# Root and reciprocal taken on one number per token and head, in the key and the group normalisation

## The reference, cut to what matters

```python
hs = lambda u: u.reshape(b, t, RWKV_HEADS, RWKV_HEAD)
kk = hs(k * k_k)
kk = kk * lax.rsqrt(jnp.maximum(jnp.sum(kk * kk, -1, keepdims=True), 1e-24))   # key normalisation
...
mu_y = y.mean(-1, keepdims=True)                                               # y: output of the scan
var_y = jnp.square(y - mu_y).mean(-1, keepdims=True)
y = ((y - mu_y) * lax.rsqrt(var_y + GN_EPS)).reshape(b, t, RWKV_DIM) * lnx_g + lnx_b   # group normalisation
```

## Time and profile before

| | us |
|---|---|
| median of 3 runs | 4569.9 |
| the three runs | 4568.84, 4569.9, 4578.2 |
| the profiled execution, its own time | 4578.92 |
| its span | 4577.1 |
| `project_pairs` early, late | about 145 to 305, 1160 to 1555 |
| `scan_pairs` early, late | about 305 to 560, 1555 to 2190 |
| busy: PE, DVE, ACT, POOL | 3770.9, 3228.8, 883.7, 1830.5 |

### The profile page before, as it was taken

The page is one execution under the profiler, slowest core; times in us unless marked ns, Lnnn a source line. Parts: engine busy times, 40 slices in busy tenths (PEclk is TensorE's granted clock), DMA queues, the critical chain, the costliest instruction groups (busy, mean ns, idle before and its releaser), DMA issues. The chain is left out here.

```text
span 4577.1 us, 70268 instructions
## 1 busy us (share of the span) xinstructions
PE 3770.9 (82%) x27402; PEld 2494.4 (54%) x27402; DVE 3228.8 (71%) x6034; ACT 883.7 (19%) x1778; POOL 1830.5 (40%) x1489
## 2 busy tenths in 40 slices
PE   7876788899888587777778785766999999999997
PEld 6666665555445476776554354553554445444543
DVE  0555422568889577776777658984889888977778
ACT  1332220110222222222441011661000000000000
POOL 0016000057212033331325305853656665666664
PEclk9988789899989798888779887767999999999998
DMA  7552343399899566665559742447999999999997
GB/s 170 165 153 86 122 160 128 117 337 404 207 208 206 169 199 231 209 214 166 170 177 373 310 176 42 79 107 301 405 407 398 405 397 406 388 398 407 404 406 280
DMA packets 438542, 1154.49 MB, mean 252 GB/s; under 512 B 84497, under 2 KB 179260, under 8 KB 434588
## 3 DMA queue, kind: packets, MB, share of 16 engines
q0 software_dynamic: 207216, 687.87, 43.3%
q1 hardware_dynamic: 194564, 422.08, 26.9%
q10 hardware_dynamic: 36432, 40.05, 2.6%
HBM read 1045.72 MB, written 114.70 MB: 254 GB/s over the span
## 5 line engine op out<-in xcount | busy, mean ns | idle before, releaser
L2646 PE MATMUL x_sps<-c_big,l_c_wo 128*128 128x384 f32 x2048 | 689.4, 499 | 91.3 <-DMA l_c_wo<-u_cols 80.9
L381 POOL DMA_INDIRECT l_w_ring<-u_rows,k_eidx x256 | 299.2, 1169 | 986.6 <-DVE l_w_dots L437 454.3
L2653 PE MATMUL x_vps<-x_v,x_w 128*128 128x512 f32 x1536 | 662.3, 592 | 3.1 <-DVE x_w L2686 3.1
L381 POOL DMA_INDIRECT w_ring<-u_rows,k_eidx x384 | 480.8, 1252 | 443.6 <-DVE w_dots L437 282.7
L2646 PEld LDWEIGHTS x_sps<-c_big,l_c_wo 128*128 128x128 f32 x2048 | 399.8, 196 | 381.2 <-DMA l_c_wo<-u_cols 87.0
L454 DVE SCALAR_TENSOR_TENSOR w_yacc<-w_ring,w_wts,w_yacc 128x1024 f32<-128x1024 f32 x384 | 493.4, 1285 | 54.7 <-DMA w_ring<-v_rows,k_eidx 42.6
L2653 PEld LDWEIGHTS x_vps<-x_v,x_w 128*128 128x128 f32 x1536 | 291.7, 190 | 367.7 <-issue 357.8
L437 DVE CUSTOM_DVE_ANT_0 w_ring<-w_ring,w_h 128x1024 f32<-128x1024 f32 x384 | 452.3, 1224 | 52.1 <-DMA w_ring<-u_rows,k_eidx 27.0
L381 POOL DMA_INDIRECT w_ring<-v_rows,k_eidx x384 | 426.0, 1109 | 133.2 <-issue 113.0
L381 POOL DMA_INDIRECT l_w_ring<-v_rows,k_eidx x256 | 289.3, 1130 | 372.1 <-DVE l_w_yacc L454 319.6
L454 DVE SCALAR_TENSOR_TENSOR l_w_yacc<-l_w_ring,l_w_wts,l_w_yacc 128x1024 f32<-128x1024 f32 x256 | 329.0, 1285 | 52.0 <-DMA l_w_ring<-v_rows,k_eidx 43.9
(11 more groups left out here) (634 smaller groups left out, 6198.1 us busy)
## 6 DMA issues: line engine op xcount, KB each, us to landing
l_c_wo<-u_cols SPq DMA_DIRECT2D x128, 512.0 KB, 6.9
x_v<-v_rows SPq DMA_DIRECT2D x128, 512.0 KB, 11.8
e_c_w<-w_tiles SPq DMA_DIRECT2D x54, 512.0 KB, 3.9
l_c_w<-w_tiles SPq DMA_DIRECT2D x54, 512.0 KB, 7.7
l_c_wo<-s_G SPq DMA_DIRECT2D x16, 1536.0 KB, 23.2
s_rw<-l_q_out SPq DMA_DIRECT2D x48, 384.0 KB, 13.7
s_G<-l_f_stage ACTq DMA_DIRECT2D x8, 2048.0 KB, 7.8
s_zT<-l_pz ACTq DMA_DIRECT2D x30, 384.0 KB
```

The lines of the kernel that those rows point to most:

```text
L381: pool.indirect_dma_start(out=self.ring[:, r, :], out_offset=None, in_=self.A[table], in_offset=bass.IndirectOffsetOnAxis(ap=idx[:, s:s + ...
L2646: mm = pe.matmul(sps[n % 2][:, 0:ND * P], u[n % 4][:, k, :], hT[:, k, :], start=(k == 0), stop=(k == KT - 1))
L2653: mm = pe.matmul(vps[k][:, x * 512:(x + 1) * 512], w[:, e, k * P:(k + 1) * P], v[:, e, x * 512:(x + 1) * 512], start=(c == 0 and e == 0), ...
```

## The change

Both sums are now made with the tokens on the partitions: the squares are the stationary operand, in runs of up to 128 tokens, and two columns of `bd` the moving one, so that a run gives a 128 x 2 result (token by head). The maximum or addition, the root and the reciprocal work on that small tile (`norm`: 12 columns for a late pair, 6 for a tail of 384 tokens, two pieces for the 264 columns of an early pair). A new step `rb` spreads it out again: a product whose stationary operand is a column of `norm` broadcast to 64 columns and whose moving operand is the identity, one for each run and head, into PSUM; the multiplication reads it there. In `project_pairs` the step `rb` stands behind the projection V in PE's list, ACT's root moves ahead of its three exponentials and DVE's `ssm` ahead of the vectors of r. In `scan_pairs` the tables get a place for `rb`, and scale and gate move one chunk or two later.

```diff
-    PE = Steps("w", "a", "g", "r", "ss", "v", "bonus", *only("raw_t", "dec_t"))
-    AC = Steps("w", "a", "g", "r", "Dinv", "D", "Dprev", *only("wdec"), "norm", "v", *only("raw_t"))
+    PE = Steps("w", "a", "g", "r", "ss", "v", "rb", "bonus", *only("raw_t", "dec_t"))
+    AC = Steps("w", "a", "g", "r", "norm", "Dinv", "D", "Dprev", *only("wdec"), "v", *only("raw_t"))
+    runs = [(o, min(P, pt.N - o)) for o in range(0, pt.N, P)]
...
-                pe.wait_ge(act_done, AC.after("g", p))
                 pe.wait_ge(dve_done, DV.after("sq", p))
-                small(1, bd[:, :], sq[:, :])
+                for i, (o, m) in enumerate(runs):
+                    mm = pe.matmul(sums[0:m, 2 * i:2 * i + 2], sq[:, o:o + m], bd[:, 0:P:HD], start=True, stop=True)
+                mm.then_inc(pe_done, 1)
...
                 project(Q_PAIR_V, 0, pe_done)
-                pe.wait_ge(dve_done, DV.after("ssm", p))
+                pe.wait_ge(dve_done, DV.after("rinv", p))
+                for i, (o, m) in enumerate(runs):
+                    for h in range(2):
+                        mm = pe.matmul(rb[h * HD:(h + 1) * HD, o // GN, o % GN:o % GN + m], norm[0:m, 2 * i + h:2 * i + h + 1].broadcast_to([m, HD]),
+                                       ident[0:m, 0:m], start=True, stop=True)
+                mm.then_inc(pe_done, 1)
+                pe.wait_ge(act_done, AC.after("g", p))
                 small(1, bd[:, :], rk[:, :])
...
-                dve.wait_ge(pe_done, PE.after("ss", p))
-                do("ssm", V.tensor_scalar(pt.grouped(sq[:, :]), zp[1][:, :, 0:GN], 1e-24, None, ALU.max))
                 dve.wait_ge(act_done, AC.after("norm", p))
-                do("rinv", V.reciprocal(sq[:, :], sq[:, :]))
-                do("kk", V.tensor_tensor(kk[:, :], kkr[:, :], sq[:, :], ALU.mult))
+                for rows, cols in whole:
+                    ins = V.reciprocal(norm[rows, cols], norm[rows, cols])
+                do("rinv", ins)
+                dve.wait_ge(pe_done, PE.after("rb", p))
+                do("kk", V.tensor_tensor(pt.grouped(kk[:, :]), pt.grouped(kkr[:, :]), rb[:, :, 0:GN], ALU.mult))
...
-    TAIL1 = {1: ("mean",), 2: ("var",), 3: ("ri",), 4: ("scale",), 5: ("gate",)} if NC > 5 else {1: ("mean",), 2: ("var",), 3: ("ri", "scale", "gate")}
-    TAIL0 = {MID + 1: ("mean",), MID + 2: ("var",), MID + 3: ("ri", "scale"), MID + 4: ("gate",)} if NY == 2 else {}
+    TAIL1 = {1: ("mean",), 2: ("var",), 3: ("ri",), 4: ("rb",), 5: ("scale",), 6: ("gate",)} if NC > 6 else {1: ("mean",), 2: ("var",), 3: ("ri", "rb", "scale", "gate")}
+    TAIL0 = {MID + 1: ("mean",), MID + 2: ("var",), MID + 3: ("ri",), MID + 4: ("rb",), MID + 5: ("scale", "gate")} if NY == 2 else {}
...
-                    pe.matmul(tps[:, 0:HT], bd[:, :], sqy[:, :], start=True, stop=True).then_inc(pe_tail, 1)
+                    for i in range(HT // P):
+                        mm = pe.matmul(sums[:, 2 * i:2 * i + 2], sqy[:, i * P:(i + 1) * P], bd[:, 0:P:HD], start=True, stop=True)
+                    mm.then_inc(pe_tail, 1)
+                if step == "rb":
+                    need(p, f"ri{g}")
+                    for i in range(HT // P):
+                        for h in range(2):
+                            mm = pe.matmul(tps[half(h), i * P:(i + 1) * P], norm[:, 2 * i + h:2 * i + h + 1].broadcast_to([P, HD]),
+                                           ident[:, :], start=True, stop=True)
+                    mm.then_inc(pe_tail, 1)
...
-                    do("tv", V.tensor_scalar(sqy[:, :], tps[:, 0:HT], 1.0 / HD, GN_EPS, ALU.mult, ALU.add))
+                    do("tv", V.tensor_scalar(norm[:, :], sums, 1.0 / HD, GN_EPS, ALU.mult, ALU.add))
-                    do("ri", V.reciprocal(sqy[:, :], sqy[:, :]))
+                    do("ri", V.reciprocal(norm[:, :], norm[:, :]))
-                    do("yn", V.scalar_tensor_tensor(y, y, of_pair(C_LG), sqy[:, :], ALU.mult, ALU.mult))
+                    dve.wait_ge(pe_tail, PT_.after(f"rb{g}", p))
+                    do("yn", V.scalar_tensor_tensor(y, y, of_pair(C_LG), tps[:, 0:HT], ALU.mult, ALU.mult))
```

More of the change, by code:

```diff
@@ L655, in project_pairs @@
     only = lambda *names: names if dec else ()
-    PE = Steps("w", "a", "g", "r", "ss", "v", "bonus", *only("raw_t", "dec_t"))
-    AC = Steps("w", "a", "g", "r", "Dinv", "D", "Dprev", *only("wdec"), "norm", "v", *only("raw_t"))
+    PE = Steps("w", "a", "g", "r", "ss", "v", "rb", "bonus", *only("raw_t", "dec_t"))
+    AC = Steps("w", "a", "g", "r", "norm", "Dinv", "D", "Dprev", *only("wdec"), "v", *only("raw_t"))
     DV = Steps("k_d", *only("k_ds"), "k_f", "kkr", "sq", "lw", "scan", "lprev", "a", "ka1", "kp",
-               "r_d", *only("r_ds"), "r_f", "rkr", "rk", "ssm", "rinv", "kk", "kka", "v_d", *only("v_ds"), "v_f",
+               "ssm", "r_d", *only("r_ds"), "r_f", "rkr", "rk", "rinv", "kk", "kka", "v_d", *only("v_ds"), "v_f",
                "alpha", "beta", "kappa", "rho", "dend", "betae", "kappae", *only("dec_t0", "dec_t1"))
+    runs = [(o, min(P, pt.N - o)) for o in range(0, pt.N, P)]
     n, N, NG, GN, GZ, ZW, z0, NC = pt.n, pt.N, pt.ng, pt.gn, pt.gz, pt.zw, pt.z0, pt.NC
@@ L692, in project_pairs @@
         zp = [ctx.enter_context(nc.psum_tensor(pt.tag + f"qzp{j}", [P, NG, 512], F32)) for j in range(2)]
-        tp = [ctx.enter_context(nc.psum_tensor(pt.tag + f"qtp{j}", [P, 512], F32)) for j in range(2)]
+        tp = [ctx.enter_context(nc.psum_tensor(pt.tag + f"qtp{j}", [P, 512], F32)) for j in range(2)] if dec else None
+        rb = ctx.enter_context(nc.psum_tensor(pt.tag + "qrb", [P, NG, 512], F32))
+        sums = ctx.enter_context(nc.psum_tensor(pt.tag + "qsums", [P, 512], F32))
+        norm = sb("q_norm", [P, 2 * len(runs)])
+        whole = [(slice(0, P), slice(0, 2 * (N // P)))] + ([(slice(0, N % P), slice(2 * (N // P), 2 * len(runs)))] if N % P else [])
         const_in, lora_in = sem("q_const_in"), sem("q_lora_in")
@@ L853, in _ @@
                     shift(Q_PAIR_R, p)
-                act.wait_ge(dve_done, DV.after("lprev", p))
+                act.wait_ge(dve_done, DV.after("ssm", p))
+                for i, (rows, cols) in enumerate(whole):
+                    ins = act.activation(norm[rows, cols], norm[rows, cols], ACT.Sqrt)
+                ins.then_inc(act_done, 1)
                 act.activation(Di[:, :], lcum[:, :], ACT.Exp, scale=-1.0).then_inc(act_done, 1)
@@ L860, in _ @@
                     act.activation(wdec[:, :], tw[:, DEC], ACT.Exp).then_inc(act_done, 1)
-                act.wait_ge(dve_done, DV.after("ssm", p))
-                act.activation(sq[:, :], sq[:, :], ACT.Sqrt).then_inc(act_done, 1)
                 act.wait_ge(pe_done, PE.after("v", p))
@@ L935, in _ @@
                 bg.dve(dve, 4 * plan["pair"])
+                dve.wait_ge(pe_done, PE.after("ss", p))
+                for rows, cols in whole:
+                    ins = V.tensor_scalar(norm[rows, cols], sums[rows, cols], 1e-24, None, ALU.max)
+                do("ssm", ins)
                 dve.wait_ge(act_done, AC.after("r", p))
@@ L1054, in scan_pairs @@
     PP, PC = Steps(*order), Steps(*chain)
-    PT_ = Steps(*[f"{x}{g}" for g in range(NY) for x in ("mean", "var")])
+    PT_ = Steps(*[f"{x}{g}" for g in range(NY) for x in ("mean", "var", "rb")])
     AP, AC = Steps(*[x for x in order if on_act[x]]), Steps(*[f"Y{g}" for g in range(NY)], *(["fin"] if final else []))
@@ L1087, in scan_pairs @@
         ps = [psum(f"r_ps{j}", 512 * NY) for j in range(2)]
+        norm = sb("r_norm", [P, 2 * HT // P])
         ups, sps, yps, tps = psum("r_ups", 512), psum("r_sps", 512), psum("r_yps", 512), psum("r_tps", 512)
+        sums = tps[:, HT:HT + 2 * HT // P]
         side.banks(psum)
@@ L1208, in tail @@
                     if g:
-                        need(p, f"tv{g - 1}")
+                        need(p, f"yn{g - 1}")
                     elif p:
@@ L1266, in _ @@
             tail("var", NY - 1, NPAIR - 1)
+            tail("rb", NY - 1, NPAIR - 1)
         @block.scalar
@@ L1288, in tail @@
                     act.wait_ge(dve_tail, DT.after(f"tv{g}", p))
-                    act.activation(sqy[:, :], sqy[:, :], ACT.Sqrt).then_inc(act_tail, 1)
+                    act.activation(norm[:, :], norm[:, :], ACT.Sqrt).then_inc(act_tail, 1)
             def turn(p, j, more):
```

## The result

The changed kernel took 4517.25 us (median of 4 runs, 4498.88 to 4525.03) against 4572.35; ratio 0.9872, 95% interval 0.984 to 0.9904. Timed again on another chip, where the kernel before took 4594.3, the ratio was 0.9869 (0.9853 to 0.9885). The profiled execution took 4525.03 us, its span is 4523.2.

What follows compares the result with a forecast made beforehand. Late scan was taken as bound by the chain PE to DVE and back, late pairs by DVE's period. 0 - 3 - 6 - 36 = -45 gave 4534 from the profiled 4578.9, 4525 from the median; middle 4530, range 4500 to 4561.

Steps and rivals of the forecast that it cites:

- Late project_pairs: Late pairs: period from kk to kk 42.45 us in place of 44.14, -6 in all, bounds -46 and +16.
- the weights come late: Rival, late pairs: a shorter period brings more weight stalls of about 8 us each, three giving up to 4555; 10%.
- rb is dear: Rival: rb's broadcast-column instructions cost more than 0.113 us each, the gain gone at about 0.215; 8%.
- Early project_pairs: Early pairs: PE's list sets the period, about 16.1 us after 16.27; sum 0, bounds -15 and +9.
- Late scan, chunks 9 to 11: Late scan_pairs: reciprocal gains 2.4 us, multiplications moved behind the last state 1.9, with 3.5 of room there; 4.3 a turn.
- Chunk 8: Late scan_pairs: the smaller tv gives 0.4 us a turn and shorter sums up to 0.2 more.
- Chunks 3 to 6: Late scan_pairs: rb adds 1.36 us to a full PE in chunk 4, less smaller waits, so +0.5 a turn.
- Chunk 7: Late scan_pairs: the prediction had no term for this chunk.
- Early scan: Early scan_pairs: +0.5 us a turn for the exchange, against one long DVE lock gone; sum -3, bounds -10 and +8.
- The lock: Early scan: yn's multiplication of two SBUF tiles held 8.91 us beside POOL; about 9 us goes, 3 to 4 comes back.
- the clock stays up: Rival, late scan chunks 9 to 11: PE waits less and keeps its clock, perhaps 2 us a turn, giving 4516; 15%.
- The 9 us between profiled run and median: Profiled run lies 9.0 us above the median; likely its one weight stall, which cost DVE about 8.

Runs made afterwards that it cites:

- e12: e9 with the products of rb in project_pairs issued twice, the second time with the same values; 4521.83 us, ratio 0.9882.
- e1: Changed project_pairs with the scan_pairs of the kernel before; 4575.86 us, ratio 1.0007.
- e2: Changed scan_pairs with the project_pairs of the kernel before; 4503.43 us, ratio 0.9843.
- e3: Kernel before with its large reciprocal, only the late scan's multiplications and gates moved to later chunks; 4559.29 us, ratio 0.9961.
- e4: Changed kernel with the late scan's multiplications and gates left in their old places; 4534.67 us, ratio 0.9913.
- e9: Changed kernel with the weights of the next pair's K asked for ahead of the stores; 4519.57 us, ratio 0.9857.
- e7: Changed kernel without background expert work beside the late pairs, done in later stages instead, for timing alone; 4579.21 us, ratio 0.9965.
- e5: Changed kernel as it is, timed again on another chip; 4533.92 us, ratio 0.9869.
- e8: e2 without background expert work beside the late pairs, done in later stages instead, for timing alone; 4579.0 us, ratio 0.9963.
- e6: Changed kernel with rb's products inside the last group of V's stream, sums and reciprocal on DVE reordered to suit; 4523.45 us, ratio 0.9845.

## Why the prediction came out

4530 in 4500 to 4561 was predicted, 4517 came. The mechanism of the late scan was right. That the sum is this near is in part luck: between the profiled executions the gain is 53.9 where 45 was forecast, and the early scan gave 7 more than forecast, the late scan 5 more and the early pairs 3 more, while the late pairs gave 5 less. Term by term (in the late scan as the mean of turns 1 to 6, from U to U):

- *Late project_pairs, -6.* It failed. The cadence was better than predicted, 41.2 and not 42.45, because I took 0.113 us an instruction for `rb` from the earlier trace rows, where 1.53 us for 24 instructions and the doubling in `e12` show 0.054 to 0.067. But the stall, held to be the same 8 as before, grew by 12.7. The seven intervals came to -1.6, the first `kk` 1.0 later, the stage to -0.6; by the medians of `e1` and `e2` it is worth nothing or costs time. The rival *the weights come late* had the mechanism, though it cost one stall of 20 and not several of 8, and what is late need not be the weights. The doubling also rules out *rb is dear*.
- *Early project_pairs, 0.* -3.1: the first to the last `kk` took 110.9 us and not 113.9. This is within its bounds; PE's list set the period, as forecast, and was shorter by the lower price of `rb`.
- *Late scan, chunks 9 to 11, -4.3 a turn.* -3.3. The 4.3 from the reciprocal to the last state came exactly; 0.9 came back in chunk 11, where the multiplications delay the next turn's first U, so the room behind the last state was smaller than the 3.5 read from the earlier trace rows. `e3` shows the same +0.9.
- *Chunk 8, -0.6.* +0.4; other traces with the changed scan have -0.4 to +0.4. *Chunks 3 to 6, +0.5.* +0.4, but not by its parts: chunk 4, which was to grow by 1.36 for `rb`, grew by 0.1, chunk 3 with the smaller reciprocal shrank by 1.9, and chunk 5, where the multiplications now stand, grew by 1.7.
- *Chunk 7, nothing.* -2.5 a turn, the largest miss of the scan. Before, PE stops there in the middle of a stream without a wait that the profile names. The waits in one such chunk of 9.1 us:

```profile
PE l_r_ps L1193 <- issue: 2.6, 2, 1.8
DVE c_big L1340 <- PE l_r_ps L1193: 1.4, 1, 1.4
```

  Over turns 1 to 6 these pauses are 2.2 us a chunk before, 1.6 in `e1` with the same scan, 0.6 in `e3`, 1.3 in `e4`, 0.1 after. Why they go when the tails move isn't settled. Chunks 0 to 2 give another -0.8, and the last turn -1.2 where I had -3. Sum of the late scan: -40.7, predicted -36.
- *Early scan, -3.* -10.2 in the profiled pair; eleven traces with the changed scan take 193.5 to 205.9 us, three without 211.6 to 220.5. The lock left `yn`: it took 3.61 us before and 9.10 in `e3`, and is never stretched in the eleven traces where it reads PSUM. The Trainium skill ("GPSIMD Engine Reference", Key points) has the contention for DVE instructions with two SBUF inputs. The traces agree: in all fourteen every stretched DVE instruction of this stage is of that form. But other instructions of two SBUF operands are stretched in its place (`ya` 8.38 in `e9`). All stretching together is 27.4 us before, 27.0 in `e3`, 18.3 to 23.8 with the changed scan, and also 22.4 in `e1`, whose `yn` still reads SBUF and happened to run free. So it is worth 5.8 of the 10 in this pair of traces, and `e1` shows that part of this is chance. The rest is in the ordinary turns, which I had at +0.5: from the last state to the next U stand 2.8 us and not 3.6, and the granted clock is higher. One whole turn, before and after:

```profile
476.40:501.15 24.75, 22.09 (x517) 20.01 (x517) 11.12 (x27) 7.10 (x19) 0.00 (x0) 0.86 0.18 54
```
```profile
468.57:489.92 21.35, 19.29 (x507) 17.48 (x509) 9.27 (x26) 6.91 (x19) 0.00 (x0) 1.00 0.24 62
```

  The granted clock is 1.00 and not 0.86, and PE's busy time 2.8 less. All eleven traces with the changed scan have this turn at 21.3 to 21.4 us and 1.00, `e1` has it at 24.7 and 0.86. In `e3`, whose early scan is that of before, it took 23.4 at 0.93, so 1.3 us can come with the clock and no change of code. That is the rival *the clock stays up*, in the other scan than I had put it; the late one went from 0.87 to 0.88 only.
- *The 9 us between profiled run and median*, put down to the stall: not borne out. The profiled run of `e3` has no stall and lies 7 above its median, that of `e1` has one of 13 and lies 12 below.

## What to carry to other kernels

A shorter instruction on the busiest engine is worth what the chain of that stage gives: 2.4 us off a chain paid in the scan, 5 us off DVE paid nothing in a stage whose DMA share is 0.96, and nothing in `e7` either, where PE was full. Put an exchange with another engine a step ahead of its use. Judge two edits that touch one chain together: alone they gave 17 and 11 us of the 41. Where a stage's transfers fill it, ask how late they come at the new cadence before counting the gain.

## What the runs showed of the hardware

- A product with a stationary column broadcast over 64 and an identity of 128 columns takes 0.054 to 0.067 us an instruction where it stands in the path, about half of the 0.113 that the earlier trace rows give for 128 x 128 weights by 128 columns.
- An early turn in which DVE's part from last state to next U was 0.8 us shorter became 3.4 shorter, 2.8 of it PE's busy time at a granted clock of 1.00 in place of 0.86. No run separates the clock from the shorter DVE part, apart from the 1.3 us of `e3`.
- On the chip of `e5` to `e8` the same late scan took 545.2 us in `e5` (546.3 in `e6`) against 523.2, with chunks 4 and 5 each 1.6 longer, DVE busy alike (386.6) and PE's "issue" waits more and shorter (42 and not 13 at the batches). The kernel before was slower there too, 4594.3 against 4574. Why isn't known.
